# Moving weight loads, waits, small tables and one head's evacuation in a hybrid decoder step, and rounding the first chunk of a pair at a block's half

## The reference

```
h = rmsnorm(x); proj = h @ w_in                       # 2048 -> 1024 (pool) + 4 x 1024 (q, k, v, gate)
a = pool_mix(...)                                     # 4 groups, causal means over 2, 4, 8, 16 tokens, 256x256 map
b = retention(...)                                    # 4 heads of 256: rotary, decay, states, head norm, silu gate
x = x + concat(a, b) @ w_out
x = x + mem_attn(rmsnorm(x), mk, mv, w_mq, w_mo)      # mk, mv from rmsnorm(mem) @ w_mk, w_mv; 4 heads of 512
x = x + peer(rmsnorm(x), ...)                         # 8 heads, product keys 128 x 128, top 16 of 16384 experts,
                                                      # sum over experts of softmax * gelu(u . x) * v
y = rmsnorm(x)
```

## Time and profile before

| | |
|---|---|
| median of 3 runs | 4538.81 us (4538.28 to 4539.96) |
| profiled execution | 4544.36 us, its span 4542.6 us |
| PE, PE weight load | 96%, 91% of the span busy |
| POOL, DVE, ACT | 61%, 48%, 34% |
| mean granted TensorE clock | 0.989 of full speed |
| DMA | 1032 MB, mean 227 GB/s |

### The profile page before, as it was taken

One profiled execution on the slowest core, in us unless ns is written; L12 is line 12 of the kernel. 1 busy time (PEld: TensorE's weight loads), 2 busy tenths in 40 slices (PEclk: granted clock), 3 DMA queues, 4 the chain that ended last, 5 costly groups with the idle time before them and its releaser, 6 DMA issues.

```text
span 4542.6 us, 75520 instructions
## 1 busy us (share of the span) xinstructions
PE 4381.2 (96%) x28787; PEld 4141.9 (91%) x28787; DVE 2177.9 (48%) x3231; ACT 1525.1 (34%) x1921; POOL 2774.2 (61%) x1440
## 2 busy tenths in 40 slices
PE   7999999999999989999999998999999999999998
PEld 7899989899888978888888998999999999999998
DVE  3132333423102153333333565777777777777656
ACT  4422222222222244444443553333333333333332
POOL 6833222243222457777777887788788788886643
PEclk9999999999999999999999999999999999999999
DMA  6643333434564255555555559999999899999854
GB/s 228 209 95 100 111 111 106 155 105 146 196 203 168 88 177 183 182 182 181 181 181 183 187 188 341 350 359 353 354 355 358 320 357 363 358 356 347 324 190 157
DMA packets 493934, 1032.09 MB, mean 227 GB/s; under 512 B 55776, under 2 KB 285280, under 8 KB 461024
## 3 DMA queue, kind: packets, MB, share of 16 engines
q1 hardware_dynamic: 316528, 592.77, 39.9%
q0 software_dynamic: 45056, 268.60, 15.2%
q10 hardware_dynamic: 132208, 168.75, 10.7%
HBM read 935.26 MB, written 94.73 MB: 227 GB/s over the span
## 4 chain that ended last, share of the span: by engine, by line
PE 49%; issue 24%; POOL 17%; DMA 6%; ACT 2%; DVE 1%; POOLq 0%; ACTq 0%; SPq 0%; DVEq 0%
PE PS L598 21%; PE PS L948 15%; POOL WS L484 14%; PE PS L1045 12%; DMA RAW<-in_vE 6%; POOL AR L507 2%; ACT WS L1080 1%; POOL ROWS L517 1%; PE PS L974 0%; DMA ROWS<-in_vE,AR 0%; DMA AR<-gel 0%; DVE AR L1759 0%; DVE AR L2266 0%; PE PS L1001 0%; DVE HL L1782 0%
## 5 line engine op out<-in xcount | busy, mean ns | idle before, releaser
L598 PE MATMUL PS<-HL,WS 128*128 128x288 f32 (+2 forms) x16896 | 2394.9, 303 | 66.6 <-POOL WS L484 35.2
L598 PEld LDWEIGHTS PS<-HL,WS 128*128 128x128 f32 x16896 | 2351.7, 190 | 87.3 <-issue 30.5
L484 POOL TENSOR_TENSOR WS<-RAW,WS 128x1024 fp32r<-128x1024 f32 x600 | 1458.0, 2439 | 1418.8 <-ACT WS L1080 1416.5
L1080 ACT ACTIVATE WS<-RAW 128x1024 fp32r<-128x1024 f32 x600 | 614.8, 1055 | 1190.1 <-PE PS L598 451.6
L1045 PE MATMUL PS<-WW,WS 128*128 128x320 f32 x6144 | 927.0, 312 | 56.5 <-POOL WS L484 44.8
L1045 PEld LDWEIGHTS PS<-WW,WS 128*128 128x128 f32 x6144 | 908.6, 189 | 73.6 <-issue 36.1
L948 PE MATMUL PS<-WS,HL 128*128 128x512 f32 x3072 | 700.4, 389 | 0.0
L948 PEld LDWEIGHTS PS<-WS,HL 128*128 128x128 f32 x3072 | 575.5, 188 | 118.8
L484 POOL TENSOR_TENSOR WS<-CS,WS 128x1024 fp32r<-128x1024 f32 x200 | 482.7, 2414 | 146.9 <-ACT WS L1080 145.1
L2135 DVE SCALAR_TENSOR_TENSOR PS<-ROWS,AR,PS 128x2048 f32<-128x2048 f32 x206 | 483.3, 2346 | 9.0 <-DMA ROWS<-in_vE,AR 8.7
L2150 DVE TENSOR_TENSOR AR<-AR,PS 128x320 f32<-128x320 f32 x512 | 247.1, 483 | 317.9 <-PE PS L1045 316.7
(11 more groups left out here) (220 smaller groups left out, 2274.0 us busy)
## 6 DMA issues: line engine op xcount, KB each, us to landing
RAW<-in_uT SPq DMA_DIRECT2D x256, 512.0 KB, 4.6
RAW<-in_w_lin SPq DMA_DIRECT2D x216, 512.0 KB, 3.6
CS<-in_uT SPq DMA_DIRECT2D x128, 512.0 KB, 4.7
AR<-in_uT SPq DMA_DIRECT2D x128, 512.0 KB
RAW<-in_vE SPq DMA_DIRECT2D x128, 512.0 KB, 7.9
CS<-in_vE SPq DMA_DIRECT2D x64, 512.0 KB, 4.8
AR<-in_vE SPq DMA_DIRECT2D x64, 512.0 KB
AR<-in_w_lin SPq DMA_DIRECT2D x48, 512.0 KB, 4.2
```

Source lines behind the costliest of these rows:

```text
L484: pool.tensor_tensor(WS[:, k, 1, :], raw(k, many, late), WS[:, k, 0, :].bitcast(F32), ALU.subtract)\
L598: ins = mm(to, WS[:, slot + hf, wp, k * P:(k + 1) * P], x, start=first and (wp, xp) == (0, 0), stop=last and wp == 1, skip_group_check=True)
L1080: copy = lambda out, in_, **kw: act.activation(out, in_, ACT.Identity, **kw)
```

## The change

SP: chunks 4 to 11 are loaded in pairs with one of the four token loads behind each pair; then chunks 12 to 23, and only then the rotary tables. ACT: the wait for the key stores stands behind the first eight roundings of the values' stage; the padded tables are issued at the end of pooling group 1; block 0 of head 0 is evacuated ahead of the loop over the heads, and block 0 of head h+1 at the end of head h, behind the root and ahead of the wait for `b_done`. In `ups`, `gelu_out` rounds the first chunk of the pair when PE has finished the first half of the block, and the second after Gelu as before.

```diff
@@ -328,9 +328,9 @@
 
             return v[:, :, TP + 4 * SQ * r:TP + 4 * SQ * (r + 1)].rearrange("p c (q x) -> p c q x", q=4)
 
-        def load_x(eng, src):
-
-            for q in range(4):
+        def load_x(eng, src, parts=range(4)):
+
+            for q in parts:
                 eng.dma_start(X[:, 4 * q:4 * q + 4, :], src[4 * q:4 * q + 4].rearrange("k p t -> p k t"))\
                     .then_inc(S[f"in_x{q}"], 16)
 
@@ -363,12 +363,14 @@
             for dst, src in ((CST[:, :, :], consts[:, 0:256].rearrange("p (a n) -> p a n", a=2)),
                              (RC[:, :], consts[:, 256:272])):
                 sp.dma_start(dst, src).then_inc(S["in_const"], 16)
-            load_x(sp, xT)
-            for n in range(4, 8):
+            for n in range(4, 12):
                 load(n, n % 4, w_lin[n:n + 1], many=True)
+                if n % 2:
+                    load_x(sp, xT, (n // 2 - 2,))
+            load_lin(12, 24, many=True)
             sp.wait_ge(S["t_ready"], KB)
             sp.dma_start(CS[:, :, :], rot).then_inc(S["in_rot"], 16)
-            load_lin(8, H_RET, many=True)
+            load_lin(24, H_RET, many=True)
             load_lin(H_RET, H_MQ + 8)
 
 
@@ -1194,8 +1196,6 @@
                     token_root(1)
             for m in (14, 15):
                 store_keys(m)
-            for s in range(2):
-                act.wait_ge(S[f"out_k{s}"], 128)
             for m in range(4):
                 s = m % 2
                 for q in range(8):
@@ -1204,6 +1204,9 @@
                     high(n - q % 2 + 4, q % 4 // 2 * 2, q % 2)
                     if q % 2:
                         high_part(16, 4 * m + q // 2, HALF, HALF)
+                if m == 0:
+                    for k in range(2):
+                        act.wait_ge(S[f"out_k{k}"], 128)
                 if m >= 2:
                     act.wait_ge(S[f"out_v{s}"], 16)
                 for t in range(2):
@@ -1240,14 +1243,17 @@
             pool_weights(0)
             pool_states(0)
             act.wait_ge(S["x_added"], 1)
-            for b in range(SB):
-                r, q = b // 4, b % 4
-                rows = slice(32 * q + SQ * r, 32 * q + SQ * (r + 1))
-                act.dma_start(ZM[rows], tabs[:, SQ * b:SQ * (b + 1), T_ZETAS + b - r:T_ZETAS + b - r + 2].rearrange("h p n -> p h n"))\
-                    .then_inc(S["in_pad"], 16)
-                act.dma_start(DECP[rows, :, SQ * r:SQ * (r + 1)],
-                              tabs[:, SQ * b:SQ * (b + 1), T_DECS + SQ * b:T_DECS + SQ * (b + 1)].rearrange("h p n -> p h n"))\
-                    .then_inc(S["in_pad"], 16)
+
+            def pad_tables():
+                for b in range(SB):
+                    r, q = b // 4, b % 4
+                    rows = slice(32 * q + SQ * r, 32 * q + SQ * (r + 1))
+                    act.dma_start(ZM[rows], tabs[:, SQ * b:SQ * (b + 1), T_ZETAS + b - r:T_ZETAS + b - r + 2].rearrange("h p n -> p h n"))\
+                        .then_inc(S["in_pad"], 16)
+                    act.dma_start(DECP[rows, :, SQ * r:SQ * (r + 1)],
+                                  tabs[:, SQ * b:SQ * (b + 1), T_DECS + SQ * b:T_DECS + SQ * (b + 1)].rearrange("h p n -> p h n"))\
+                        .then_inc(S["in_pad"], 16)
+
             for g in range(GROUPS):
                 for c in range(2):
                     for odd in range(2):
@@ -1269,6 +1275,8 @@
                 for c in range(2):
                     act.dma_start(npoolT_p[2 * g + c], PEX[:, c, TP:TP + BUF]).then_inc(S["out_pool"], 16)
                     act.dma_start(npoolT_s[2 * g + c], PSX[:, c, :, SQ:SQ + BUF]).then_inc(S["out_pool"], 16)
+                if g == 1:
+                    pad_tables()
 
             def pad_values(c, s):
 
@@ -1315,7 +1323,6 @@
                 for b in range(SB):
                     act.dma_start(SST[:, b], sret[b, bass.ds(h, 1)].rearrange("a (c p) v -> p (a c) v", p=P))\
                         .then_inc(S["in_st"], 16)
-                evac_head(h, 0)
                 act.wait_ge(S["vt_done"], h + 1)
                 copy(VTOK[:, 0:4, :], PS[:, 2048:3072].rearrange("p (t n) -> p t n", t=4))
                 copy(VTOK[:, 4, :], bank(6, RD)).then_inc(S["v_evac"], 1)
@@ -1346,6 +1353,8 @@
                     store_states(h, 0, 4)
                 act.wait_ge(S["rvar_ready"], h + 2)
                 act.activation(RSD, RVAR, ACT.Sqrt).then_inc(S["rsd_ready"], 1)
+                if more:
+                    evac_head(h + 1, 0)
                 if not more:
                     store_states(h, 4, SB)
                 act.wait_ge(S["b_done"], h + 2)
@@ -1370,6 +1379,7 @@
                 if s == 0:
                     pool_out(GROUPS - 1)
             act.wait_ge(S["out_a"], 16 * GROUPS)
+            evac_head(0, 0)
             with act.Fori(0, RH - 1) as h:
                 retention(h, True)
             retention(RH - 1, False)
@@ -1539,12 +1549,18 @@
                 act.dma_start(gelg[:, :, bass.ds(h * (4 * P * UPQ) + 4 * P * j, 4 * P)].rearrange("s p e -> p s e"),
                               GOG[:, e]).then_inc(S[f"out_gg{e}"], 16)
 
-            def gelu_out(r, n, e):
-
+            def gelu_out(r, n, e, at_half=False):
+
+                if at_half:
+                    act.wait_ge(S["used"], n + used(1))
+                    high(n + 4, 2 * e, late=True)
                 act.wait_ge(S["used"], n + used(2))
                 act.wait_ge(S[f"out_g{e}"], r * 16 + 16)
                 act.activation(GO[:, e, :], bank(e, ND), ACT.Gelu).then_inc(S["lin_evac"], 1)
-                high2(n + 4, 2 * e, late=True)
+                if at_half:
+                    high(n + 4, 2 * e, 1, late=True)
+                else:
+                    high2(n + 4, 2 * e, late=True)
 
             def store_gelu(r, m, e):
                 act.wait_ge(S["lin_evac"], m + 3)
@@ -1635,7 +1651,7 @@
                             store_map(last, 12, 16, "out_r1")
                         if first and (a, e) == (1, 0):
                             store_map(last, 24, 28, "out_r3")
-                        gelu_out(r + a, n + (4 * a + 2 * e), e)
+                        gelu_out(r + a, n + (4 * a + 2 * e), e, at_half=True)
                         store_gelu(r + a, m + (2 * a + e), e)
                         if first and (a, e) == (0, 0):
                             for sem_of_map, stores in (("out_p0", 272), ("out_p1", 272), ("out_m0", 16)):
```

## The result

| | before | after |
|---|---|---|
| median of 5 runs each, same chip | 4538.81 us (4536.88 to 4547.76) | 4518.19 us (4510.89 to 4521.02) |
| ratio, 95% interval | | 0.9944, 0.9928 to 0.9960 |
| profiled execution, span | 4544.36, 4542.6 | 4510.89, 4509.1 |
| start of the second expert quad | 2843.59 | 2800.67 |
| period of the quads behind it, mean of 25 | 59.09 | 59.46 |

It is faster by 0.4 to 0.7%, some 25 us by the ratio (20.6 by the two medians), where 66.9 were forecast; 4518 lies 18 us above the end of the range. Lines stand two or more lower in the changed kernel: L598 is L600 there, L1045 L1047, L484 L486, L1080 L1082, L2150 L2166.

What follows compares the result with a forecast made beforehand. TensorE, busy 96%, was taken as the bound, so only closing its gaps pays. Terms 14.7 + 4.1 + 5.1 + 13.0 + 30 = 66.9 us took the median from 4538.8 to 4472, range 4456 to 4500.

Steps and rivals of the forecast that it cites:

- Step 1: Kernel start: weight chunks requested ahead of the token loads close early TensorE gaps and cold clock, 14.7 us (5 to 16).
- Step 2: Values' stage: waiting for key stores behind eight roundings removes TensorE's 1.90 us stall and cold clock, 4.1 us (0 to 4.5).
- Step 3: Pooling: issuing the 16 table DMAs later lets ACT round sooner and removes a 3.66 us stall, 5.1 us (3 to 5.1).
- Step 4: Retention heads: evacuating each head's block 0 earlier removes three TensorE gaps and cold clock, 13.0 us (8 to 13).
- Step 5: Expert quads 1 to 25: rounding at the block's half closes the first gap and shortens the second, 30 us (0 to 44.8).
- I take 1.4 of the 2.1: Quads: of 2.1 us gained on POOL, 1.4 was assumed to become earlier chunk landing, giving 1.2 us per quad.
- The row at 1.04: Quads' down stage: DMA engines shown full at 411 GB/s, so only part of the 2.1 us would become earlier landing.
- the single stretch at 0.92: DMA share just before the down stage, taken as evidence against engines so full that an earlier request wins nothing.
- My lower bound: Quads: if nothing lands earlier, quarter 2 loses what quarter 0 gains, 0 us.
- Rival (a): Quads: DMA engines bound the second gap, landings stay, quads give 0 to 8 us, time 4494 to 4502; chance 0.17.
- The 2.1 us on POOL: Quads: rounding at the half removes POOL's idle 0.85 and 1.23 us, so chunks 8 and 9 come 2.1 us earlier.

Runs made afterwards that it cites:

- the run with half rows: The changed kernel with each gathered row fetched at 1024 values instead of 2048, 5.2 MB less per quad, sums left wrong; 4442.35 us, ratio 0.9780.

## Why the prediction was wrong, by its steps

**Step 1, the start: 14.7 forecast, 12.3 measured** (the values' stage starts at 116.56 instead of 128.83). The mechanism was right in each gap. What was off is the clock: I ran block 2 at the warm rate from 29.1. In after PE was granted 0.50 from 21.3 to 25 and 0.71 to 29, behind the same 1.87 us wait after which before had 1.00; so the 111 matmuls from 21.30 took 16.19 and not 13.2, and the stage began at 45.38, not 43.8.

```profile
21.30:25.00 3.70, 3.70 (x17) 0.50 0.85 286
25.00:29.00 4.00, 4.00 (x27) 0.71 0.64 247
29.00:33.00 4.00, 4.00 (x35) 1.00 0.72 186
```

**Step 2, key stores: 4.1 forecast, 3.8 measured** (from the values' start to 203.63 are 87.07, before 90.87). **Step 3, tables: 5.1 forecast, 5.5 measured** (first head at 360.74 instead of 382.32, less the 16.1 before). **Step 4, heads: 13.0 forecast, 13.3 measured** (34.8 at the last head, less 21.6). In the profile steps 1 to 4 sum to 34.9; in timed runs they are 31.7 (25 to 37 by the interval of the ratio). The profiled pair shows 42.9 at the second quad's start. Of the 8 beyond 34.9, 6.6 arose between the last head and the first quad, where the change does nothing: PE is idle there for 36.0 us before and 36.7 after, and busy for 1878.1 and 1870.9, so they are clock and not the change (last section). The other 1.5 are in the first quad.

**Step 5, quads: 30 forecast; measured -9.4 in the profile (1486.6 us for the 25 quads against 1477.2), -6.4 with the half alone.** This is the step that failed, in the sentence "I take 1.4 of the 2.1". Up to the request for chunk 12 everything came as worked out, here on the mean of the 25 quads: chunk 8 is 2.2 earlier into the quad (20.6 against 22.9), the requests for chunks 12 and 13 2.2 earlier, the first gap gone. Then the request became no earlier landing: of 2.2 us 0.9 at chunk 12 (36.0 against 36.9) and -0.2 at chunk 13 (40.7 against 40.5), on which quarter 2 waits; it starts at 44.45 instead of 44.55. The kernel with the half alone repeats this, with 40.8 and 44.45. The row at 1.04 was the one that counted, and the single stretch at 0.92, 5 us long, on which I set the 1.4, was not: it ends at 3335, and chunk 12 was asked for at 3338.3, or 3336.1 with the 2.2 us gained. From there to the landings the engines were full before already:

```profile
3335.00:3340.00 5.00, 5.00 (x36) 1.00 0.99 350
3340.00:3345.00 5.00, 4.39 (x30) 1.00 1.05 417
3345.00:3350.00 5.00, 5.00 (x37) 1.00 1.01 402
```

In after the DMA share is 0.97 over the first 23 us of the quad and 0.99 to 1.04 from there to 3439, with one stretch of 5 us at 0.85 in it (3415 to 3420, around the request), of which nothing came back at chunk 13. The map and Gelu loads, asked for just ahead of chunk 12, are what stands in its way (the runs with late loads); the row gathers are another part of it (the run with half rows).

My lower bound was 0, since quarter 2 would lose what quarter 0 gains, and so far it held: quarter 2 starts 0.1 us sooner into a quad, 2.5 us in 25. What I had at nothing is the clock behind the one gap that grows, 1.19 to 2.05 us on the mean. The 96 matmuls of quarters 2 and 3 took 11.9 us more in after, summed over the quads (ten times half-cold against three, 1.5 us each and 1.2 more in one): 11.9 - 2.5 = 9.4. Rival (a), with 0.17, had the mechanism, landings that stay, and came out with the wrong sign because it had no term for the clock. How much of chunk 13's way each of the transfers ahead of it takes is not settled, only that there are too many bytes.

The 2.1 us on POOL was right as a number (2.2 measured at chunk 8), but 0.85 of it was never needed: where landings don't bind, chunk 8's 1.23 us closes the first gap of 0.61 and the rest is slack.

**What the forecast didn't look for** is the useful one: in that full stretch 1.31 MB were asked for ahead of chunks 12 and 13 that nobody needed for a quad. With them behind down quarter 1, 23 of the 25 quads run in 56.9, the other two, with a further step in them, in 58.7, and the whole kernel takes 4453 us, 66 less than the changed one and 88 less than before (ratio 0.9806); with the half at chunk 8 alone it is 4451, not told apart from that. Of the 88, some 32 are parts 1 to 4 and the rest is the quads (25 x 2.08 = 52 by the periods).

## What to carry to other kernels

Before an earlier request is booked as an earlier landing, look at the DMA share over the whole stretch from request to landing: if it is full, an earlier request buys nothing, and the gain lies in what is asked for ahead of it and could be asked for behind. Two short gaps and one longer gap cost different amounts on TensorE (0.63 and 1.19 us were followed by half-cold matmuls in 3 of 25 quads, one of 2.05 in 10), so an edit that merges gaps must be priced with the clock behind them. Compare means over all rounds of a loop: one pair of quads had chunk 13 0.8 us later, the mean of 25 0.2. An edit that was worth -6 us became worth +20 once the resource behind it was free: a change that fails is to be tried again after the next bound has moved.

## What was not expected of the hardware

- The clock behind a gap is not a function of the gap. Behind 1.87 us, 0.50 was granted in after and 1.00 in before; in the kernel with only the half, whose code there is that of before, the same 63 matmuls took 10.48 us instead of 7.96. In the tokens' stage, the same wait of 3.4 us is followed by 24 matmuls in 3.42 (after) and in 6.04 (before, at 894.60). Before quarter 2 of after, 2.44 is followed by 96 matmuls in 14.33 and 2.24 by 15.87. From quad 2 to quad 11 of after the two alternate, 14.33 in each even quad and 15.87 in each odd one, with gaps of 2.2 to 2.7 before both:

```profile
3380.65 14.33 PE L1047 MATMUL PS<-WW,WS 128*128 128x320 f32 x96 [2.44 <-POOL WS L486]
```

```profile
858.52 3.42 PE L600 MATMUL PS<-HL,WS 128*128 128x288 f32 x24 [3.42 <-DVE HL L1813]
```

```profile
894.60 6.04 PE L598 MATMUL PS<-HL,WS 128*128 128x288 f32 x24 [3.39 <-DVE HL L1797]
```

- One profiled run can't carry a difference under some 10 us: before and the kernel with only the half, whose code is the same up to the quads, reached one product of the memory stage at 1599.93 and 1589.62. Of these 10.3 us 6.4 are idle time of PE and 3.9 busy time, so clock; the two can't be told apart fully, since a cold stretch shortens the wait behind it (block 2 starts at 32.22 in both, behind 3.08 and 0.61 us of idle time). That the two profiles are from different chips isn't ruled out. Timed, one kernel's runs spread over 10 us with the gap of 2.4 us in each quad (4510.89 to 4521.02), and over 2.3, 3.8, 5.1 and 6.8 in the four runs in which it is gone (late loads, loads behind the fourth block, half rows, half at chunk 8), with four or five executions each.
